# Fourier mixing by folded cosine and sine transforms with split operands, in a one-layer diffusion backbone

## What is computed

```python
uf = u.reshape(B, T, N_FGROUPS, FGROUP_CH).astype(jnp.float32)
four = jnp.real(jnp.fft.fft2(uf, axes=(1, 3), norm="ortho")).astype(x.dtype)
four = jnp.einsum('btgc,gcd->btgd', four, w_four).reshape(B, T, FOURIER_DIM) * jax.nn.silu(gate_b)
y_b = four @ w_proj_b
merged = jax.nn.sigmoid(mg_a) * y_a + jax.nn.sigmoid(mg_b) * y_b
x = x + gate[:, None] * (merged @ w_out)
```

## Time and profile before

| | us |
|---|---|
| median of 3 runs | 2136.9 |
| lowest, highest | 2135.2, 2141.3 |
| the profiled execution | 2130.8 |
| its span in the trace | 2129.0 |
| TensorE matmul busy | 1993.8 (94% of the span) |
| VectorE busy | 1091.8 (51%) |
| ScalarE busy | 908.8 (43%) |
| GpSimd busy | 488.2 (23%) |
| DMA queue of SP and ScalarE | 404.9 MB, 55.5% of 16 engines |
| chain that ended last: TensorE, VectorE, DMA | 66%, 6%, 3% |

### The profile page before, as it was taken

The page is one execution under the profiler, slowest core; times in us unless marked ns, Lnnn a source line. Parts: engine busy times, 40 slices in busy tenths (PEclk is TensorE's granted clock), DMA queues, the critical chain, the costliest instruction groups (busy, mean ns, idle before and its releaser), DMA issues.

```text
span 2129.0 us, 32939 instructions
## 1 busy us (share of the span) xinstructions
PE 1993.8 (94%) x11793; PEld 1864.4 (88%) x11793; DVE 1091.8 (51%) x1858; ACT 908.8 (43%) x1895; POOL 488.2 (23%) x282
## 2 busy tenths in 40 slices
PE   6799999999999999999999799888859999999997
PEld 1799999999999999999998777777659999997886
DVE  3889888764444335444432255566793222224332
ACT  3454667744454664445452267675421010102222
POOL 0323322322332122233210000013351111111122
PEclk9899999999999999999999899999989999999999
DMA  6477778877787877688887485541333434454533
GB/s 261 156 265 251 279 282 310 301 252 230 264 285 263 283 288 241 225 269 287 259 290 302 157 342 218 218 175 57 123 127 100 123 116 125 123 181 142 170 126 119
DMA packets 170129, 456.94 MB, mean 215 GB/s; under 512 B 13648, under 2 KB 81546, under 8 KB 161932
## 3 DMA queue, kind: packets, MB, share of 16 engines
q1 hardware_dynamic: 156172, 404.90, 55.5%
q10 hardware_dynamic: 13824, 50.34, 5.9%
HBM read 299.99 MB, written 145.76 MB: 209 GB/s over the span
## 4 chain that ended last, share of the span: by engine, by line
PE 66%; issue 6%; DVE 6%; DMA 3%; POOL 2%; ACT 2%; SPq 0%; POOLq 0%; ACTq 0%; DVEq 0%
PE bank L1749 36%; PE bank L1942 18%; PE bank L1827 3%; PE bank L1846 1%; PE bank L1848 1%; PE bank L1847 1%; PE bank L1834 1%; DMA x_st<-in_x 1%; POOL h_lo L810 1%; DVE zb L480 1%; DMA x_in<-in_x 1%; DVE uf L1584 1%; PE bank L1855 1%; PE bank L1686 1%; PE bank L1773 1%
## 5 line engine op out<-in xcount | busy, mean ns | idle before, releaser
L1749 PE MATMUL bank<-h_hi,w_op 128*128 128x384 f32 x4032 | 1055.3, 337 | 18.1 <-DVE u L1321 6.8
L1749 PEld LDWEIGHTS bank<-h_hi,w_op 128*128 128x128 f32 x4032 | 732.6, 188 | 22.0 <-issue 22.0
L1749 PE MATMUL bank<-h_lo,w_op 128*128 128x384 f32 x2016 | 675.4, 335 | 0.0
L1749 PEld LDWEIGHTS bank<-h_lo,w_op 128*128 128x128 f32 x2016 | 380.1, 189 | 0.0
L1266 DVE TENSOR_TENSOR w_op<-w_raw,w_op 128x512 fp32r<-128x512 f32 x240 | 197.4, 824 | 125.1 <-ACT w_op L943 121.6
L1942 PE MATMUL bank<-in_hi,pw_hi 128*128 128x256 f32 x864 | 245.9, 285 | 12.2 <-DVE in_lo L1609 12.2
L1942 PE MATMUL bank<-in_lo,pw_hi 128*128 128x256 f32 x864 | 245.7, 284 | 0.0
L1942 PE MATMUL bank<-in_hi,pw_lo 128*128 128x256 f32 x864 | 245.7, 284 | 0.0
L943 ACT ACTIVATE w_op<-w_raw 128x512 fp32r<-128x512 f32 x240 | 150.3, 627 | 164.6 <-PE bank L1749 152.6
L1942 PEld LDWEIGHTS bank<-in_hi,pw_hi 128*128 128x128 f32 x864 | 167.2, 193 | 12.4 <-issue 12.4
L829 POOL TENSOR_TENSOR decs<-decs,qk_s 128x768 f32<-128x768 f32 x48 | 92.6, 1951 | 368.0 <-ACT decs L1017 368.0
(11 more groups left out here) (211 smaller groups left out, 2931.5 us busy)
## 6 DMA issues: line engine op xcount, KB each, us to landing
w_op<-wt_dram SPq DMA_DIRECT2D x192, 512.0 KB, 5.7
wt_dram<-w_op ACTq DMA_DIRECT2D x96, 512.0 KB, 4.4
w_raw<-in_w_in SPq DMA_DIRECT2D x48, 768.0 KB, 6.1
w_raw<-in_w_in SPq DMA_DIRECT2D x24, 1024.0 KB, 6.7
qk_dec<-decs SPq DMA_DIRECT2D x48, 384.0 KB, 7.2
mg_dram<-outs SPq DMA_DIRECT2D x24, 768.0 KB, 7.1
mg_ld<-mg_dram SPq DMA_DIRECT2D x72, 256.0 KB, 2.9
swap<-qk_s SPq DMA_DIRECT2D x48, 192.0 KB, 6.3
```

Of the source, the lines that this page charges most:

```text
L1749: ins = pe.matmul(bnk, w_op[slot][:, part, k, :], h[:, j, k, :], start=(first and k == 0 and part == 0 and h is h_hi), stop=(k == HK - 1 a ...
```

## The change

- Instead of radix butterflies and twiddles, the positions are folded about their middle: GpSimd forms sums and differences of position t and N - t, then folds the even part again about its middle and once more, 18 instructions in all, 12 of which read one operand backwards. What is left are real cosine and sine transforms of 512 positions (odd outputs) and 256 positions (even outputs), done with tables `tab_o` and `tab_e` on TensorE in split form (high and low, three float32r matmuls). The context is folded once and uses plain float32.
- The channel products have 128 columns per group (only a cosine or only a sine part). ScalarE writes the high part, VectorE the low part. `cw` is made before the attention.
- Nine items (`ITEMS`) follow: four odd ones (24 matmuls of 512 columns each), the context, four even ones (24 of 256 columns). For each, ScalarE copies the cosine half, VectorE forms sum and difference with the sine half; the sum gives the output row k, the difference row N - k. VectorE multiplies the first by the gate, GpSimd the second, in place in `ym`, which holds the gates.
- The weights come by output tile: `w_proj` is stored as 8 tiles of 128 x 12 x 128. GpSimd makes the lows of tiles 0 to 2, VectorE those of 3 to 7. Tiles 3 and 4 are loaded after item 3, 5 to 7 at the end of the items. The first branch matmul waits for the attention part of block 0, and each output tile for its own weights. In a block, the Fourier part of tile j - 1 follows the attention part of tile j.
- SBUF is laid out anew by explicit offsets.

The core of the diff:

```diff
+ITEMS = [("odd", 3), ("odd", 2), ("odd", 1), ("odd", 0), ("ctx", None), ("even", 3), ("even", 2), ("even", 1), ("even", 0)]
...
+        FOLDS = [7] * 4 + [11] * 4 + [5] * 2 + [15] * 4 + [18] * 4
...
SP:
+                        sp.dma_start(w4[:, :, :], io["w_four"]).then_inc(s_ctab, 16)
+                        sp.dma_start(chan[:, :, :], io["chan"]).then_inc(s_ctab, 16)
                     load_summed(n + 1, 6)
...
-                    sp.dma_start(w4[:, :, :], io["w_four"]).then_inc(s_ctab, 16)
-                    sp.dma_start(dft[:, :, :, :], io["dft"]).then_inc(s_ftab, 16)
-                    sp.wait_ge(s_p0, 3)
-                    sp.dma_start(chan[:, :, :], io["chan"]).then_inc(s_ctab, 16)
+                    sp.dma_start(tab_e_raw[:, :, :, :], io["tab_e"]).then_inc(s_ctab, 16)
...
+            sp.wait_ge(s_gt, NT * HEADS)
+            for n in range(2):
+                sp.dma_start(tab_o_raw[:, n, :, :], io["tab_o"][:, n]).then_inc(s_tab_o, 16)
+            sp.dma_start(tab_c[:, :], io["tab_c"]).then_inc(s_tab_o, 16)
...
+            for g in range(GROUPS - 1, -1, -1):
+                if g == 0:
+                    sp.wait_ge(s_zm, FOLDED)
+                sp.dma_start(ym[:, g, :], gb_dram[g]).then_inc(s_gb, 16)
...
+            sp.wait_ge(s_zm, FOLDED + 1)
+            for j in range(3):
+                load_weights(j)
+            sp.wait_ge(s_f, 4)
+            load_weights(3)
+            for half in range(2):
+                load_og(0, half)
+            load_weights(4)
+            sp.wait_ge(s_f, len(ITEMS))
             for j in range(4):
                 load_mg(0, j)
+            load_weights(7)
+            load_weights(6)
+            sp.wait_ge(s_fo, len(ITEMS) + 2)
+            sp.wait_ge(s_fp, len(ITEMS))
+            load_weights(5)
...
GpSimd:
+            fold(he[:, :, 1:HALF], u[:, :, 1:HALF], u[:, :, HALF + 1:LAT][:, :, ::-1], ALU.add)
+            pool.wait_ge(s_ub, 1)
+            fold(u[:, :, 1:HALF], u[:, :, 1:HALF], u[:, :, HALF + 1:LAT][:, :, ::-1], ALU.subtract)
...
+            fold(eo[:, :, 1:QUART], he[:, :, 1:QUART], he[:, :, QUART + 1:HALF][:, :, ::-1], ALU.subtract)
...
+            low_table(pool, tab_o[1][:, 1, :, :], tab_o_raw[:, 1, :, :], tab_o[0][:, 1, :, :], 2, s_pwp)
+            low_table(pool, tab_e[1][:, :, :, :], tab_e_raw[:, :, :, :], tab_e[0][:, :, :, :], 3, s_pwp)
...
+            for i in range(len(ITEMS)):
+                above_middle(i)
+                j = i - 1
+                if j in LOW_POOL:
+                    pool.wait_ge(s_pwh, 3 + j + 1)
+                    pool.tensor_tensor(pw[j][1][:, :, :], pw_raw[j][:, :, :], pw[j][0][:, :, :].bitcast(F32), ALU.subtract
+                                       ).then_inc(s_pwp, 1)
...
ScalarE:
+            for m in range(FOLDED):
...
+                act.wait_ge(s_zm, m + 1)
+                act.activation(z_home(m, 0), bank[Z_BANKS[m % 4]][:, :], ACT.Copy).then_inc(s_zh, 1)
+                if m == 8:
+                    act.wait_ge(s_tab_o, 48)
+                    act.activation(alt[:, :], tab_c[:, 2 * P + 2:2 * P + 4], ACT.Copy).then_inc(s_am, 1)
+                elif m in (9, 11):
+                    n = m // 2 - 4
+                    act.activation(tab_o[0][:, n, :, :], tab_o_raw[:, n, :, :], ACT.Copy).then_inc(s_pwh, 1)
...
+            for i in range(len(ITEMS)):
+                even_part(i)
+                if 1 <= i <= 5:
+                    high_pw(i - 1)
+                elif i == 6:
+                    for half in range(2):
+                        k = slice(4 * half, 4 * half + 4)
+                        high(s_og[half], in_hi[0][:, k, :], og_ld[:, k, :], 16, s_ih)
...
VectorE:
+                dve.wait_ge(s_es, i + 1)
+                dve.tensor_tensor(s[:, :], sines[:, :], cosines[:, :], ALU.add).then_inc(s_sd, 1)
+                if i >= 2:
+                    dve.wait_ge(s_fp, i - 1)
+                dve.tensor_tensor(d[:, :], cosines[:, :], sines[:, :], ALU.subtract).then_inc(s_sd, 1)
+                dve.wait_ge(s_sd, 2 * i + 1)
+                dve.wait_ge(s_gb, 16 * GROUPS)
...
+            dve.wait_ge(s_sd, 2 * len(ITEMS))
             dve.memset(pad[:, :], 0.0).then_inc(s_yg, 8)
+            dve.wait_ge(s_fo, len(ITEMS) + 2)
+            dve.wait_ge(s_fp, len(ITEMS))
+            low_fourier(0, 0)
+            for j in range(len(LOW_POOL), 8):
+                low_pw(j)
...
TensorE:
+            for m in range(FOLDED):
+                if m >= 4:
+                    if ZT <= m - 4 < ZT + 2:
+                        pe.wait_ge(s_zh, m - 3)
+                    else:
+                        pe.wait_ge(s_zl, z_low(m - 4))
+                pe.wait_ge(s_ub, FOLDS[m])
...
+            pe.wait_ge(s_zl, ZT)
             pe.wait_ge(s_on, NT * HEADS)
+            pe.wait_ge(s_pwl, 1)
+            pe.wait_ge(s_pwp, 1)
+            item(0)
...
+                pe.wait_ge(s_il, 3 * b + 2)
+                for j in range(9):
+                    if j < 8:
+                        pe.wait_ge(s_yg, 8 * b + j + 1)
+                        if j in LOW_POOL:
+                            pe.wait_ge(s_pwp, 2 + j + 1)
+                        else:
+                            pe.wait_ge(s_pwl, 1 + j + 1 - len(LOW_POOL))
+                        part(j, range(KT), 0)
+                    if j:
+                        if j == 1:
+                            pe.wait_ge(s_il, 3 * b + 3)
+                        part(j - 1, range(KT, KA), MB).then_inc(s_y, 1)
```

More of the change, by code:

```diff
@@ new lines, in build @@
+        zc = place(153600, "zc", [P, 2, 512])
+        tab_c = place(157696, "tab_c", [P, 2 * P + 4])
+        misc = place(158752, "misc", [P, 40])
+        alt = place(158944, "alt", [P, 2], F32R)
+        cw = place(159744, "cw", [P, GROUPS, 2, P])
+        he = place(163840, "he", [P, GROUPS, HALF])
+        wc = Region(second + 4 * 2 * TOK)
+        w4, chan = wc("w4", [P, GROUPS, P]), wc("chan", [P, 2, P])
+        cos_t = [place(159744 + 2048 * n, f"cos_t{n}", [P, 512]) for n in range(2)]
@@ new lines, in _, with low_fourier @@
+            for i in range(len(ITEMS)):
+                combine(i)
+                if i == 4:
+                    middle()
+                elif i in (6, 7):
+                    half = i - 6
+                    k = slice(4 * half, 4 * half + 4)
+                    low(in_lo[0][:, k, :], og_ld[:, k, :], in_hi[0][:, k, :], s_ih, half + 1, s_il)
+            def low_fourier(b, slot):
+                low(in_lo[slot][:, KT:KA, :], ym[:, :, b * MB:b * MB + MB] if isinstance(b, int) else
+                    ym[:, :, bass.ds(b * MB, MB)], in_hi[slot][:, KT:KA, :], s_ih, 3 * b + 3, s_il)
@@ L1809, in _ @@
             pe.wait_ge(s_gc, len(use_number))
+            pe.wait_ge(s_ctab, 32)
+            for g in range(GROUPS):
+                for r in range(2):
+                    ins = pe.matmul(bank[6 + g // 2][:, 256 * (g % 2) + P * r:256 * (g % 2) + P * r + P], chan[:, r, :],
+                                    w4[:, g, :], start=True, stop=True)
+                if g % 2:
+                    ins.then_inc(s_g, 1)
+            pe.wait_ge(s_gc, len(use_number) + 2)
             def pe_head(head, n, i):
@@ new lines, in middles @@
+            def middles():
+                for g in range(GROUPS):
+                    for n in range(4):
+                        pe.matmul(bank[MISC_BANK][:, 16 + 2 * g:18 + 2 * g], z_even[:, n % 2, n // 2, P * g:P * g + P],
+                                  alt[:, :], start=(n == 0), stop=(n == 3))
+                for g in range(GROUPS):
+                    ins = pe.matmul(bank[MISC_BANK][:, 24 + 2 * g:26 + 2 * g], zc[:, 0, P * g:P * g + P], tab_c[:, 2 * P:2 * P + 2],
+                                    start=True, stop=True)
+                ins.then_inc(s_zm, 1)
```

515 lines of the change are left out of this document (265 added, 250 removed).

## The result

The changed kernel takes 2103.6 us (median of four, 2099.0 to 2107.3), the kernel before 2137.1 us: a ratio of 0.984, 95% interval 0.9815 to 0.9864. The forecast was 2101.9 in 2084 to 2124, faster. The gain is 1.6%, clear of the spread of the runs. The profiled execution of after took 2107.3 us, its span is 2105.5; that of before took 2130.8.

A forecast was written before the change was run, and what follows sets the result against it. VectorE, not TensorE, was taken to set the Fourier part's end. Attention ending at 1494 plus 71 us put the first branch matmul at 1565 instead of 1600, 35 us less: 2101.9 us, range 2084 to 2124.

The forecast's parts named there:

- The folds' length: GpSimd's folding in the last attention head: 48.4 us plus about 1.5 us for small ones, backward reads at the forward price.
- the rival that ended slower: GpSimd reads backwards at twice the price, folding lasts 98 us: branches start 13 us later, 2150 us; chance 0.08.
- T: End of the attention on TensorE: 1484 us before, forecast 1494 us, so that part costs 10 us (6 to 16).
- 5 or 6 fewer are left: Attention chunks left after the folds: 5.5 fewer at 2.5 us each, so 13.1 us remain instead of 26.9.
- the 3 us allowed for a low clock: Attention after the folds: 9 us gaps on TensorE lower its clock, adding 3 us.
- Products, table and odd items: Fourier part: table loads pace the channel products, item 0 starts at T + 22, items 0 to 3 are done at T + 49.
- The tail: Fourier part's end: ScalarE waits for weight tile 4, VectorE finishes behind it, first branch matmul at T + 71.
- the term of VectorE's own work: Fourier part's end, from item 6: three combines of 2.4 us and two lows of 1.3 us, 9.8 us.
- the rival: Items bound by VectorE and GpSimd excluding each other, 5.5 us an item: branches 20 us earlier, 2117 us; chance 0.17.
- T + 60: Early bound for the first branch matmul, if weight tile 4 lands unnoticed.
- Behind the branches: Branch product and after: unchanged, late weight tiles covered by some 9 us.
- Shared bandwidth: Folds beside VectorE's state update: sharing instead of exclusion, update perhaps 1 us, T near 1487, 7 us better; no chance given.

The follow-up runs named there:

- Weight tile 4 later: ScalarE makes the high part of weight tile 4 after the items instead of between items 5 and 6, against the changed kernel: 2101.5 us, ratio 0.984.

## Why the prediction was right, step by step

By its own terms, against the profile of after:

**The folds' length: right.** 49.9 us forecast, 49.9 measured. The forward price for a backward read was right (8.86 and 9.04 us), and with it falls the rival that ended slower.

**T: 2 us too early, by two errors.** The chunks that pass during the folds were 11, as allowed. The step that failed is "5 or 6 fewer are left". Of the 17 state updates of the forward scan, before had 7 behind it when its folds ended: 6 in the folds, as I counted, and one (1427.61 us) just ahead of them, which I left out. After had 11. So 4 fewer were left, not 5.5: 3.8 us more, 2.5 of them for the update left out and the rest for taking the middle of 11 and 12. It isn't a matter of where the first fold happens to start: in the unedited kernel's second profile and with the folds read forwards the first update comes ahead of the folds, 10 pass in them, 6 are left as well, and L is 82.1. Against that, the 3 us allowed for a low clock were too much: 26.9 - 4 x 2.5 = 16.9 us should be left after the folds, 18.1 were, 1.2 us more. In sum +12.0 where I had +10. That the clock falls in the folds (0.83 over them) was right; from 1484.7 to T it was granted in full (1.00).

**Products, table and odd items: right to 1 us.** ScalarE waits for `tab_c` at product 8 and goes on at T + 10.3 (forecast T + 11). Item 0 starts at T + 21.3 (forecast T + 22); GpSimd's `tab_o` low ends 0.1 us ahead of VectorE's last remainder, so the two end it together. Items 0 to 3 are done at T + 49.1 (T + 49), TensorE has all done at T + 62.7 (T + 62).

**The tail: on VectorE, as forecast, but 3.5 us short, for its main term was too small.** I had the branches at T + 71 and they came at T + 74.5. The landing of tile 4 (T + 59.7 by the start of its high, forecast T + 58.5) and ScalarE's last copy (T + 65.4, forecast T + 65) were right. VectorE began item 6 at T + 62.0 behind ScalarE's copy (forecast T + 61), as I had it, but it had waited for that copy only 0.68 us: it was at the context item and item 5 from T + 53. The step that failed is the term of VectorE's own work: from item 6 on I had 9.8 us (2.4 an item, 1.3 a low half), and it took 12.4 (2.9 and 1.8, start to start), because GpSimd's multiplies ran beside. I had named this exclusion in the rival and left it out of the forecast. Nor is T + 60 in reach where tile 4 goes unnoticed, as my range had it: with its high moved behind the items the branches still came at T + 72.6. Weight tile 4 later moved X by 1.9 us, of which 0.7 is the wait, and leaving out GpSimd's multiplies by 3.3 (25.3 to 22.0), which puts the tail on VectorE. The rival's 5.5 us an item (T + 82) was too much: it had each multiply wait for 1.7 us, and a pair of them was lengthened by 0.65.

**Behind the branches: right.** TensorE waits for nothing inside the branch product, and R is 528.1 against 529.0. Waiting for all tiles first would have cost 10 to 12 us.

**The sum.** 12.0 - 41.4 - 0.9 = -30.3 us by stretches, where I had -35: +2.0 from T, +3.6 from the way to the branches, -0.9 behind. The medians differ by 33.5, so the forecast of the time is off by 1.7 us where its stretches are off by 4.7: that it came so near is in part luck. T's two errors had opposite signs as well.

The rule of the Trainium skill (SBUF — State Buffer, Who interferes with whom) that a VectorE instruction with two SBUF inputs and a GpSimd instruction that reads SBUF exclude each other is borne out, for whole instructions, by three grains of the same folds: L = 82.2, 69.9 and 61.9 us with 8.9, 4.6 and 2.5 us for the longest instruction. Shared bandwidth would have made them alike. Its other rule (GPSIMD Engine Reference, Performance pitfalls for Q7 kernels), half as much again for reads beyond a step of 8 bytes, isn't contradicted: some 255 elements at a step of 16 bytes take 1.19 us each (2.38 for two), 4.7 ns an element, where 512 at a step of 8 bytes take 1.70 us, 3.3 ns. Both include turns of VectorE's, so the ratio of 1.4 is no measurement of the rule; without such a turn one multiply of 256 took 0.85 us (weight tile 4 later), and none of 512 ran so.

**What stays open.** How the 30 us of W that don't belong to the weights divide between the lighter butterflies and the folding that was moved ahead wasn't tried.

## What to carry to other kernels

Where GpSimd works beside a VectorE chain of short operations with two SBUF operands, don't ask how long GpSimd works but how long one of its instructions is: keep it under the chain's own period (2.5 us here), even if the sum grows (49.9 to 57 us here, and 20 us of the kernel's time won). When a wait is found on an engine, read whether the engine behind it was idle too: 3.12 us on ScalarE were 0.68 us on VectorE. And count the operations that are done when a stretch ends, not those that pass within it: one update just ahead of the folds, left out of the count, was worth 2.5 us of forecast.
